# A two-layer diffusion backbone step on one core: residual stream held by channels, or by tokens

## The reference

```python
def layer(x, mod, p, latent, ckv_ctx, krope_ctx, hf0, hb0):
    sh1, sc1, g1, sh2, sc2, g2 = jnp.split(mod, N_MOD, axis=-1)      # mod = silu(c) @ w_mod[l] + b_mod[l]
    h = rms_norm(x, p["g_pre_mix"]) * (1.0 + sc1) + sh1
    y, ckv, krope, hf, hb = mixer(h, p, latent, ...)                 # w_in, attention, RG-LRU, gates, then "@ w_out"
    x = x + g1 * rms_norm(y, p["g_post_mix"])
    h = rms_norm(x, p["g_pre_ffn"]) * (1.0 + sc2) + sh2
    x = x + g2 * rms_norm(swiglu(h, p), p["g_post_ffn"])             # w_ffn_in (2 x 2816), then "@ w_ffn_out"
    return x, ckv, krope, hf, hb
```

## Time and profile before

| | us |
|---|---|
| median of 3 runs (1500.94 to 1502.65) | 1501.56 |
| the profiled execution | 1498.01 |
| its span, first to last instruction | 1496.2 |
| TensorE busy (92% of the span) | 1381.5 |
| DVE busy | 769.5 |
| ACT busy | 656.0 |

### The profile page before, as it was taken

One profiled execution on the slowest core, in us unless ns is written; L12 is line 12 of the kernel. 1 busy time (PEld: TensorE's weight loads), 2 busy tenths in 40 slices (PEclk: granted clock), 3 DMA queues, 4 the chain that ended last, 5 costly groups with the idle time before them and its releaser, 6 DMA issues.

```text
span 1496.2 us, 22085 instructions
## 1 busy us (share of the span) xinstructions
PE 1381.5 (92%) x8835; PEld 1282.3 (86%) x8835; DVE 769.5 (51%) x1448; ACT 656.0 (44%) x1100; POOL 21.2 (1%) x38
## 2 busy tenths in 40 slices
PE   6899889899989999999978987988999799999995
PEld 4798789677969999999968986987789699999995
DVE  4687373753656334443187764746454744443333
ACT  3378664643333333342145867545333433333220
POOL 0000000200000000000000000020000000000000
PEclk9999999999999999999989999999999999999998
DMA  9534533314325555553224433522225355554421
GB/s 328 163 112 121 176 113 112 119 57 141 113 85 173 169 170 169 169 183 113 88 85 140 129 127 122 180 92 99 85 85 169 106 186 163 174 178 142 155 85 43
DMA packets 138379, 202.63 MB, mean 135 GB/s; under 512 B 9851, under 2 KB 68389, under 8 KB 138277
## 3 DMA queue, kind: packets, MB, share of 16 engines
q1 hardware_dynamic: 138276, 201.22, 41.3%
HBM read 199.30 MB, written 1.88 MB: 134 GB/s over the span
## 4 chain that ended last, share of the span: by engine, by line
PE 76%; DVE 10%; ACT 8%; DMA 3%; issue 2%; SPq 0%; DVEq 0%; ACTq 0%
PE bank L612 21%; PE bank L613 20%; PE bank L614 20%; PE bank L658 3%; PE bank L642 3%; DVE weight_low L1255 3%; ACT weight_high L934 2%; PE bank L851 2%; PE bank L829 1%; DMA raw<-in_w_in 1%; PE bank L651 1%; DMA raw<-in_w_o_mla 1%; PE bank L685 1%; PE bank L838 1%; PE bank L686 1%
## 5 line engine op out<-in xcount | busy, mean ns | idle before, releaser
L612 PE MATMUL bank<-act_high,weight_high 128*128 128x384 f32 x1568 | 548.0, 350 | 41.8 <-DVE act_low L1307 13.7
L614 PE MATMUL bank<-act_high,weight_low 128*128 128x384 f32 x1568 | 532.3, 339 | 0.0
L613 PE MATMUL bank<-act_low,weight_high 128*128 128x384 f32 x1568 | 531.9, 339 | 0.0
L1255 DVE TENSOR_TENSOR weight_low<-raw,weight_high 128x1024 fp32r<-128x1024 f32 (+5 forms) x282 | 319.3, 1154 | 281.1 <-ACT weight_high L934 279.9
L934 ACT ACTIVATE weight_high<-raw 128x1024 fp32r<-128x1024 f32 (+5 forms) x282 | 273.6, 995 | 296.3 <-DMA raw<-in_w_ffn_in 121.3
L612 PEld LDWEIGHTS bank<-act_high,weight_high 128*128 128x128 f32 x1568 | 300.3, 192 | 65.4 <-issue 15.8
L613 PEld LDWEIGHTS bank<-act_low,weight_high 128*128 128x128 f32 x1568 | 300.5, 192 | 1.1 <-issue 0.6
L614 PEld LDWEIGHTS bank<-act_high,weight_low 128*128 128x128 f32 x1568 | 299.9, 191 | 0.0
L612 PE MATMUL bank<-hid_high,weight_high 128*128 128x384 f32 x352 | 118.4, 336 | 0.0
L613 PE MATMUL bank<-hid_low,weight_high 128*128 128x384 f32 x352 | 117.6, 334 | 0.0
L614 PE MATMUL bank<-hid_high,weight_low 128*128 128x384 f32 x352 | 117.6, 334 | 0.0
(11 more groups left out here) (207 smaller groups left out, 1440.7 us busy)
## 6 DMA issues: line engine op xcount, KB each, us to landing
mod_weight<-in_w_mod SPq DMA_DIRECT2D x96, 512.0 KB, 4.8
raw<-in_w_ffn_in SPq DMA_DIRECT2D x176, 256.0 KB, 4.3
raw<-in_w_in SPq DMA_DIRECT2D x72, 512.0 KB, 3.9
raw<-in_w_ffn_out SPq DMA_DIRECT2D x44, 512.0 KB, 4.1
first_mod<-in_w_mod SPq DMA_DIRECT2D x4, 2048.0 KB, 14.3
raw<-in_w_o_lru SPq DMA_DIRECT2D x16, 512.0 KB, 3.7
raw<-in_w_out SPq DMA_DIRECT2D x16, 512.0 KB, 4.0
raw<-in_w_o_mla SPq DMA_DIRECT2D x8, 512.0 KB, 6.3
```

Of the source, the lines that this page charges most:

```text
L612: nc.tensor.matmul(o, view[0][:, kk, cols], high[:, k, :], start=k == 0, stop=False)
L613: nc.tensor.matmul(o, view[0][:, kk, cols], low[:, k, :], start=False, stop=False)
L614: ins = nc.tensor.matmul(o, view[1][:, kk, cols], high[:, k, :], start=False, stop=k == total - 1)
L1255: nc.vector.tensor_tensor(low, w, high.bitcast(F), ALU.subtract).then_inc(*VE.step())
```

## The change

The residual stream x is held by tokens (three tiles of 128 tokens by 1024). `w_out` and `w_ffn_out` are computed with the activations as the stationary operand and 512 weight columns streaming (`token_job`), which gives the result by tokens: 144 matmuls of 512 columns for w_out in place of 192 of 384, 396 in place of 528 for w_ffn_out. Tokens come in the order of tiles 1, 2, 0, so that the first tile is complete before the last. The sums of squares for the norms are taken by ACT along the row (`accum_out`), with no matmul. The turn back to channels is a matmul of x by a diagonal matrix of the inverse roots (`turned`), 24 for each norm ahead of a projection; the first are issued behind the projection (`turn_first`), those of chunks 5 to 7 within the next job. The gains of the two post norms are rows now: modulation blocks 4, 5, 10 and 11 aren't folded but spread over the partitions by two float32 matmuls of 512 columns each (`gain_spread`). The hosts of the modulation blocks move: 6 to 9 take the places of 4 to 7, 4 is hosted by `ol0` and 5 by `ol1` (before: 8 by `ol1`, 9 by `wo0`). The last layer leaves out blocks 0 to 3. The small parameter rows of the next layer are read early, in `gg0`, turned beside the rows of `outs`, and copied from a PSUM bank in the middle of DVE's `lru_full` loop (`par_next`). The diff, cut to its core:

```diff
-MODS = ((4, "lx1", "qk"), (5, "gg1", "m2b"), (6, "m2a", "m1b"), (7, "m1a", "ol0"), (8, "ol1", "om1"), (9, "wo0", "wo1"),
-        (10, "fi0", "fi1"), (11, "fi2", "fi3"), (0, "fi4", "fi5"), (1, "fi6", "fi7"), (2, "fi8", "fi9"), (3, "fi10", "fo0"))
+MODS = ((6, "lx1", "qk"), (7, "gg1", "m2b"), (8, "m2a", "m1b"), (9, "m1a", "qn1"), (4, "ol0", None), (5, "ol1", None),
+        (0, "fi0", "fi1"), (1, "fi2", "fi3"), (2, "fi4", "fi5"), (3, "fi6", "fi7"), (10, "fi8", None), (11, "fi10", None))
+TILES = (1, 2, 0)
...
-            if job in HOSTED and i in (0, 3):
-                mod(HOSTED[job], (0, 1) if i == 0 else (2, 3))
+            if job in HOSTED and i in (2 if job == "ol1" else 0, 3):
+                mod(HOSTED[job], (0, 1) if i < 3 else (2, 3))
...
-                 ("qn0", [(AC, "qn", 2)]), ("qn1", [(AC, "qn", 5)]), ("kn", [(AC, "kn", 3)]), ("vv", [(AC, "vv", 3)]),
+                 ("qn0", [(AC, "qn", 2), (VE, "par_next")]), ("qn1", [(AC, "qn", 5)]), ("kn", [(AC, "kn", 3)]), ("vv", [(AC, "vv", 3)]),
...
                     if n == of_job("gg0")[0]:
                         cache_rows()
+                        if l + 1 < DEPTH:
+                            vector_rows(l + 1)
+                    if n == of_job("wo")[4]:
+                        gain_rows("mix")
+                    if n == of_job("fo")[8]:
+                        gain_rows("ffn")
...
+                    if not load.split and not hosts(l, load.job[1]):
+                        continue
...
+            for a in TILES:
+                for h in range(2):
+                    half = slice(512 * h, 512 * h + 512)
+                    sp.wait_ge(*in_layer(DEPTH - 1)(VE, "x", "ffn", a, h))
...
+                    sp.dma_start(dst, x[:, a, half]).then_inc(end_store, 16)
...
+            def turned(at, pre, job, c, tiles, *label, layer):
+                for a in tiles:
+                    pe.wait_ge(*at(AC, "diag", pre, a))
+                    ins = nc.tensor.matmul(turn_bank(job, c)[:, P * a:P * a + P], x[:, a, P * c:P * c + P], rstd[:, P * a:P * a + P],
+                                           start=True, stop=True)
...
+                def gain_spread(r, job):
...
+                    for g in range(2):
+                        nc.tensor.matmul(bank(f"{job}_b", 2 + g)[:, :], sel[g][:, :], partial[PARTIAL[r]][:, :], start=True, stop=True
+                                         ).then_inc(*PE.step("spread", r, g))
...
+                def token_job(job, high, low, ready, after, begin_b):
...
+                        for kk in range(2):
+                            k = 2 * i + kk
+                            nc.tensor.matmul(o, high[:, k, toks], view[0][:, kk, :], start=k == 0, stop=False)
+                            nc.tensor.matmul(o, high[:, k, toks], view[1][:, kk, :], start=False, stop=False)
+                            ins = nc.tensor.matmul(o, low[:, k, toks], view[0][:, kk, :], start=False, stop=k == 2 * pairs - 1)
...
+                    for a in TILES:
+                        for h in range(2):
+                            for i in (pairs - 2, pairs - 1):
...
-                split_job("wo0", hh, hl, ready=(VE, "mix_low"))
...
+                token_job("wo", hh, hl, "mix_low", {0: 4, 1: 5}, lambda: pe.wait_ge(*at(VE, "mix", 5)))
+                turn_first(l, "ffn", "wo")
                 for j in range(FC // 2):
+                    split_job(f"fi{j}", hh, hl, ready=(VE, "h", "ffn") if j == 0 else None,
+                              between=turn_between(l, "ffn", "wo", {3: (5,), 11: (6,), 15: (7,)}) if j == 0 else None)
+                token_job("fo", hidh, hidl, "hid_low", {6: 10, 7: 11}, lambda: banks_free("fo_b"))
...
+                def square(src, col, *label, layer=l):
...
+                    nc.scalar.activation(squares_out[used[0] % 3], src, ACT.Square, accum_out=ss[:, col:col + 1]
+                                         ).then_inc(*AC.step(*label, layer=layer))
...
+                    for a, h in ((1, 0), (1, 1)):
+                        y(a, h)
+                    xs(1, 0)
...
+                    y(0, 1)
+                    xs(0, 0)
+                    xs(0, 1)
...
+                def residual(job, post):
...
+                    for a in TILES:
+                        y(a, 0)
+                        y(a, 1)
+                        add(a, 0)
+                        add(a, 1)
...
+                    if c == 5:
+                        mod_result(9)
+                        gain(scale2, 4, "g_pre_ffn", ("scale2",))
+                        if l + 1 < DEPTH:
...
+                            nc.vector.tensor_copy(par[:, :], bank("outs", 3)[:, 0:NA + NB]).then_inc(*VE.step("par_next"))
...
+                        else:
+                            VE.also("par_next")
...
                     if s == 12:
-                        mod_result(7)
                         mix_lru(0)
+                        mod_partial(4)
```

More of the change, by code:

```diff
@@ L485, in _ @@
                         sp.sem_inc(sync_passed, 1)
-                    layer = l if load.split or load.job[1] not in NEXT else (l + 1) % DEPTH
+                    layer = l if load.split or load.job[1] not in NEXT else l + 1
                     for part in load.parts:
@@ L917, in _ @@
             ac.sem_inc(AC.sem, 1)
+            made = [0]
+            used = [0, []]
             for l in range(DEPTH):
@@ new lines, in y_square, with x_square @@
+                def y_square(job, post, a, h):
+                    ac.wait_ge(*at(PE, job, a, h))
+                    square(token_bank(job, a, h)[:, :], 2 * a + h, "ysq", post, a, h)
+                    if h == 0:
+                        sum_bias(2 * a, 12 + a)
+                    else:
+                        root(2 * a + 1, 12 + a, 18 + a, "y_root", post, a)
+                def x_square(ready, pre, lp, a, h):
+                    if ready is not None:
+                        ac.wait_ge(*ready)
+                    square(x[:, a, 512 * h:512 * h + 512], 6 + 2 * a + h)
+                    if h == 0:
+                        sum_bias(6 + 2 * a, 15 + a)
+                    else:
+                        root(7 + 2 * a, 15 + a, 21 + a)
+                        ac.wait_ge(*last(l, AC))
+                        nc.scalar.activation(rstd[:, P * a:P * a + P], ident[:, :], ACT.Copy, scale=ss[:, 21 + a:22 + a]
+                                             ).then_inc(*AC.step("diag", pre, a, layer=lp))
@@ new lines, in mod_result, with gain_result @@
+                    o = o.rearrange("p (g c) -> p g c", c=2)
+                    bias = par[:, 4 * r:4 * r + 4].rearrange("p (g a) -> p g a", a=1).to_broadcast([P, 4, 2])
+                    nc.vector.tensor_tensor(mod[:, 4 * r:4 * r + 4, :], o, bias, ALU.add).then_inc(*VE.step("mod", r))
+                def gain_result(r, job):
+                    which = "mix" if r in GAINS["mix"] else "ffn"
+                    to, by = GAIN[which]
+                    half = slice(512 * (r % 2), 512 * (r % 2) + 512)
+                    ve.wait_ge(*at(gain_full, which))
+                    for g in range(2):
+                        ve.wait_ge(*at(PE, "spread", r, g))
+                        nc.vector.tensor_tensor(to[:, g, half], bank(f"{job}_b", 2 + g)[:, :], by[:, half], ALU.mult
+                                                ).then_inc(*VE.step())
+                    VE.also("gain", r)
@@ L1305, in low, with normalise @@
+                def normalise(pre, lp, job, next_job, dst_scale, shift, after, chunks=range(C), early=()):
+                    atp = in_layer(lp)
                     def low(c):
-                        ve.wait_ge(*at(AC, "hh", which, c))
+                        ve.wait_ge(*atp(AC, "hh", pre, c))
                         nc.vector.tensor_tensor(hl[:, c, :], t[c % 2][:, :], hh[:, c, :].bitcast(F), ALU.subtract
-                                                ).then_inc(*VE.step("h", which, c))
+                                                ).then_inc(*VE.step("h", pre, c, layer=lp))
+                    own()
+                    for c in early:
+                        ve.wait_ge(*atp(PE, "turn_sample", pre, c))
+                        shifted(pre, lp, job, dst_scale, shift, c, 1)
+                        VE.also("sample", pre, c, layer=lp)
@@ L1318, in normalise @@
-                        VE.also("hfull", which, c)
+                        for g in range(2):
+                            if g == 0 or c not in early:
+                                shifted(pre, lp, job, dst_scale, shift, c, g)
+                        VE.also("hfull", pre, c, layer=lp)
                         if c > chunks[0]:
@@ L1321, in normalise @@
                         if c in after:
-                            lows(*after[c])
+                            lows(next_job, after[c], layer=lp)
                     low(chunks[-1])
-                def y_out(job, which, gains, first):
-                    for c in range(first, first + 4):
```

(5 more changed lines are left out.)

590 lines of the change are left out of this document (339 added, 251 removed).

## The result

The changed kernel takes 1475.84 us (median of 4 runs, 1474.6 to 1481.26), the kernel before beside it 1501.25 (1499.91 to 1502.65): a ratio of 0.984, with a 95% interval of 0.982 to 0.986. The profiled execution of the changed kernel took 1474.6, its span is 1472.7 us. Against the span of before, 1496.2, that is 23.5 less; the sum of the prediction said 22.9 less. That agreement is better than the terms deserve: several are off, in both directions, and one was missing.

A forecast was written before the change was run, and what follows sets the result against it. TensorE's own time was taken as the main bound, with seams and end a chain over three engines. Gains of 80.4 us less costs of 57.5 net -22.9: 1475.1 profiled, 1478.7 median, forecast 1479 us, range 1464 to 1491.

The forecast's parts named there:

- Seams: Stretches between `wo1` or `fo1` and the next job: 8.0 us each, bounds 6 to 10, gaining 30.3 in all.
- End: End of the program after the last product: 7.4 us in place of 22.8, with 4.0 for one small store; gain 15.4.
- Mid-job sums, folds, pace, spreads: TensorE work within full stretches: sums gain 10.4 us, folds 10.8, pace 4.7; added spreads cost 16.
- Turns in the next job: 27 turns added within the jobs behind three seams: cost 8.5 us, bounds 5 to 11.
- Wait in w_out: First spread waits for `mix` 7 behind DVE's and ACT's weight parts: 2 us a layer, +4, between 0 and 8.
- `kn`: `kn` newly waits for DVE's `par_next` behind chunk 5 of `lru_full`: 5.5 us a layer, +11, bounds 0 and 15.
- Block 4 in `ol0`: Quarters 2 and 3 queue ahead of `ol1`'s first load, delaying ACT in attention: 7.5 us a layer, +15, bounds 0 and 17.
- Begin of the program: Twelve turns in `lx0` cost 2.8 us, two multiplications by the root go: +1, between -2 and +3.
- the two new waits are covered: Rival: waits at `kn` and for the `ol1` load cost nothing, the 26 us go, 1453; chance 0.24.
- the seams stay long: Rival: ACT's small steps and squares fall behind the products, seams come out at 14 us, +18, 1497; chance 0.08.
- The clock stays up: Rival: TensorE's clock does not fall in the shorter seams, 5 us less, 1474; chance 0.04.
- The slower rival: Rival: all four `ol1` loads come some 6.5 us late for ACT in attention, +37 us, 1516; chance 0.04.

The follow-up runs named there:

- Experiment 7: Changed kernel with the last matmul of each of the six banks of w_out and w_ffn_out moved to the very end: 1516.57 us.
- Experiment 3: Changed kernel with the turns inside the first job moved: chunks 4 and 5 behind the first folds, 6 and 7 behind chunk 4's first product: 1473.80 us.
- experiment 5: Rotation products moved to the banks of `vv`, against the changed kernel with parameter copy, `ol1` load and first-job turns moved: 1443.01 us, again 1439.75.
- experiments 1 and 2: Each against the changed kernel: parameter copy moved from chunk 5 to chunk 0, 1461.96 us; first `ol1` load ahead of block 4's last quarters, 1462.96 us.
- rot_banks: Changed kernel with parameter copy, first `ol1` load and first-job turns moved, plus rotation products in the banks of `vv`: 1443.01 us, again 1439.75.

## Why the prediction was right, and where it was not

The direction, the size and the main mechanisms held. By its own steps:

*Seams:* 8.0 forecast (its own terms add up to 7.8), 7.8 measured, three times; the one in front of `lx0` as well. *End:* 7.4 forecast, 5.6 measured. The chain up to the last addition took 3.2 us (1467.12 to 1470.28) for my 3.4; what failed is the 4.0 for the last store, which took 2.4, less than my lower bound of 3. Experiment 7 shows where both come from, which I had assumed.

*Mid-job sums, folds, pace, spreads:* the pieces hold. A pair of spreads takes 1.73, where I had 2.0:

```profile
427.85 0.39 PE L719 MATMUL bank<-weight_high,act_low 128*128 128x512 f32 x1
428.08 1.02 PE L699 MATMUL bank<-mod_partial,rows_a 128*128 128x512 f32 x2
428.94 1.02 PE L699 MATMUL bank<-mod_partial,rows_b 128*128 128x512 f32 x2
...
430.03 0.40 PE L718 MATMUL bank<-weight_low,act_high 128*128 128x512 f32 x1
```

(430.03 - 427.85, less two steps at 0.227.) A group of modulation products takes 1.20, where I had 1.08 to 1.10, which left out the loss of pace around it; a fold takes 0.90. From the first to the last product of w_ffn_out it was 94.85 us and is 93.11: 1.74 less. My pieces say 1.45 (pace) + 2.6 (sums) + 0.9 (the fold of block 3 that moved) - 3.46 (spreads) = 1.5. The pace of 0.227 for 512 columns holds in w_out too (428.08 - 427.85), and with it the reason to go by rows 3 and 6: with the 2.5 ns of the Trainium skill, page "TensorE: Matmul & The Clock Gate", section "Back-to-back issue gap", a step would be 0.216, and this trace doesn't agree. That section gives this gap for an isolated matmul; for a stream in which each matmul has its weight load, as here, it gives some 131 ns at 512 columns, and the 0.227 of this trace doesn't agree with that either.

*Turns in the next job:* 8.5 forecast (27 at 0.23 and 9 at 0.3 make 8.9), 2.3 measured (0.5 and 0.3 in `fi0`, 1.5 in layer 1's `lx0`, from the first product to the first modulation products). The step that failed is "27, and 0.3 behind each group": the instructions take that, but I forgot what they replace. Before, the first products waited for scaled chunks, which DVE now makes in fewer steps.

*Wait in w_out:* 4 forecast, 2 a layer; 0.7 a layer measured: from `om0` to the last product of w_out 3.1 us less a layer, where the other pieces say 3.8 (sums 2.6, two folds 1.8, one block's products 2.4, pace 0.5, less 3.5 of spreads).

*`kn`:* the mechanism as told, DVE's copy at 290.0 for a `kn` that could go earlier; 11 forecast, 14 by removing it. The term was sized too small in three places. I took off 2.4 us of `kn`'s own waits, but 1.43 of them lie ahead of the 273.94 from which I counted the 7 us; only the second one, 0.95, lies behind it. In layer 0, counted from `qn0`, DVE came to chunk 5 another 1.7 us later than before, since ACT waited 2.67 us for the load of w_kv_up, where it had waited 0.95. And behind the wait of 9.29 us the first six products of `kn` start 0.43 apart, not 0.23: the clock is at its lower level there (0.50 from 290 to 293).

*Block 4 in `ol0`:* the mechanism as told, even to the numbers: ACT starts on the load 7.0 us after the end of the products (317.9), where I had 7.2. 15 forecast, 13 by removing it.

*Begin of the program:* +1 forecast, +7.4 measured, outside my bounds of -2 to +3. The failed step is "the twelve turns in `lx0` cost 2.8 us, two multiplications by the root go". I priced TensorE's instructions and DVE's, but not the chain. DVE makes the low part of a chunk behind the scaling of the next one, in strict order. So the turn of chunk 6, which stands 4 products ahead of its own use, holds back the products of chunk 5, which stand right behind it: it is done at 58.67, DVE scales chunk 6 and makes the low part of chunk 5 by 60.04, and TensorE, which waited 1.42 us, goes on at 60.09. The turn of chunk 7 does the same to chunk 6, 1.51 us. And the 12 turns in the middle of `lx0`, 1.26 us, push back the products of the second modulation blocks, on which the second half hangs; they start at 43.0 to 43.6 in the six traces with the old places and at 40.85 before. Experiment 3 takes 5 of the 7 away.

*Missing from the list:* the exchange of banks of `ol0`, 3.0 + 3.9 us from `kn` to the first scores, 4 to 5 in all by experiment 5. I had looked up who shares banks for `kn`, because its line is in the diff, and not for the jobs whose neighbours move without a line.

Too little cost in the begin (6.4), the banks (6.9) and `kn` (3), too much in the turns (6.2), w_out (2.6), spreads (2.2), `ol0` (2), and too little gain at the end (1.8), in the seams (0.7) and in the last layer's products (0.8): some 16 us one way and 16 the other. Each is good to about 1 us. So the forecast came out right partly by chance: by the terms alone it could have been off by 16. Of the rivals, *the two new waits are covered* is refuted by experiments 1 and 2, *the seams stay long* by the table. *The clock stays up* is half true: in two of the three seams of this trace it did, in none of the second trace of the same kernel. The slower rival didn't occur: of the four loads of `ol1` only the first was late.

## What to carry to other kernels

A change that moves work wins or loses by what each moved piece stands in front of in a strict queue. Here two harmless steps, a copy of parameters at chunk 5 and two loads ahead of another, cost 27 us of the some 80 that the rest had won, and with them and a few turns moved the kernel is 2% faster again. When buffers are given out by position in a list, print who follows whom before and after: an entry more or less changes neighbours that no line of the diff names. And a norm in another layout is only short if its parts are ready at different times: the same instructions with all tiles ready at once made seams of 18.5 to 19.2 us, no shorter than what they replaced.

## What the runs showed of the hardware

The clock of TensorE falls or doesn't at the same place of the same kernel. In the traced execution shown above the seam behind w_out takes 7.75 us at a granted clock of 1.00. This is the same seam of the same kernel in its second traced execution, busy time by stretch (columns as in rows 2), then turns and first product:

```profile
458.80:467.35 8.55, 5.68 (x32) 5.09 (x31) 4.99 (x9) 6.99 (x19) 0.00 (x0) 0.78 0.00 0
...
464.37 3.33 PE L600 MATMUL bank<-rstd,x 128*128 128x128 f32 x14 [2.28 <-ACT rstd L1116]
467.35 0.67 PE L638 MATMUL bank<-act_high,weight_high 128*128 128x384 f32 x1
467.82 0.52 PE L639 MATMUL bank<-act_low,weight_high 128*128 128x384 f32 x1
```

Behind the same wait of 2.28 us the 14 turns take 1.90 in the one and 3.33 in the other, and the next job starts at 1.2 in place of 2.4 GHz. The seam is 0.8 us longer, the following job another 1.5. Such places add up to 10 us over the program (spans 1472.7 and 1482.8, mean clocks 0.970 and 0.960). Two medians of one kernel lay 2.8 and 3.3 us apart (changed kernel, rot_banks), and a step worth 3.7 us a layer in its place was seen there at once, but in the total only when it was run again. At this size the distance of two points in the trace is the better measure, if the points take in what follows: 1.3 of the 3.7 were lost again behind the second point.
